# Dilated attention: each half of a query tile scored against its own three key tiles

## What is computed

```python
DILATED_GROUPS = ((128, 1), (512, 4), (2048, 16))   # window, dilation
for gi, (win, dil) in enumerate(DILATED_GROUPS):
    q, k, v = (to_residue(qkv[:, :, gi, n], dil) for n in range(3))
    o, lse = banded_attention(q, k, v, slopes, dil, win // (2 * dil), BLOCK_B)
wts = softmax(stack(lses), axis=0)
o = sum over the groups of wts * o, then  o @ w_out
# banded_attention: query t sees keys s with |s - t| <= window, logit bias -slope * dist_unit * |s - t|
```

## Time and profile before

| | |
|---|---|
| timed runs | 3117.51, 3118.22, 3127.80 us; median 3118.22 |
| profiled execution, its own time | 3128.69 us |
| its span | 3126.9 us |
| mean granted TensorE clock | 0.966 |
| busy over the span | PE 93%, PEld 75%, DVE 60%, ACT 41%, POOL 26% |
| the changed stage (785 to 1176 us) | 391 us, PE busy 379.5 us |

### The profile page before, as it was taken

The page is one execution under the profiler, slowest core; times in us unless marked ns, Lnnn a source line. Parts: engine busy times, 40 slices in busy tenths (PEclk is TensorE's granted clock), DMA queues, the critical chain, the costliest instruction groups (busy, mean ns, idle before and its releaser), DMA issues. The chain is left out here.

```text
span 3126.9 us, 54380 instructions
## 1 busy us (share of the span) xinstructions
PE 2899.3 (93%) x22377; PEld 2345.1 (75%) x22377; DVE 1873.7 (60%) x2647; ACT 1271.7 (41%) x1624; POOL 805.4 (26%) x461
## 2 busy tenths in 40 slices
PE   9899999999999989999979899769899799999994
PEld 8467888799777777888858677558786478888883
DVE  3766562201444445665256957685664779989997
ACT  3644332222333334332244321513222267777775
POOL 2013444344222212444400000010100024444531
PEclk9999999999999999999989899879999799999997
DMA  4633422322111112222222100321103379999996
GB/s 167 250 116 121 94 97 102 131 95 94 68 68 55 68 41 95 97 105 94 94 94 96 54 26 8 129 93 40 34 31 120 129 278 360 364 366 364 373 372 261
DMA packets 83393, 441.15 MB, mean 141 GB/s; under 512 B 19712, under 2 KB 22784, under 8 KB 34816
## 3 DMA queue, kind: packets, MB, share of 16 engines
q1 hardware_dynamic: 73920, 429.89, 37.7%
q0 software_dynamic: 9280, 8.43, 0.8%
HBM read 423.56 MB, written 37.77 MB: 148 GB/s over the span
## 5 line engine op out<-in xcount | busy, mean ns | idle before, releaser
L85 POOL TENSOR_TENSOR ring_lo<-ring,unit_hi 128x2048 fp32r<-128x2048 f32 x110 | 507.1, 4610 | 1066.1 <-ACT unit_hi L74 1066.1
L146 PE MATMUL wide<-h_hi,unit_hi 128*128 128x512 f32 x1296 | 515.6, 398 | 12.3 <-DVE h_lo L566 5.0
L147 PE MATMUL wide<-h_lo,unit_hi 128*128 128x512 f32 x1296 | 506.9, 391 | 0.0
L148 PE MATMUL wide<-h_hi,ring_lo 128*128 128x512 f32 x1296 | 506.6, 391 | 0.0
L3309 DVE TENSOR_TENSOR ex_w_lo<-ring,ex_w_hi 128x2048 fp32r<-128x2048 f32 x194 | 441.8, 2288 | 42.5 <-ACT ex_w_hi L3304 40.4
L3304 ACT CAST ex_w_hi<-ring 128x2048 fp32r<-128x2048 f32 x194 | 369.3, 1908 | 110.3 <-DMA ring<-in_weights 92.7
L74 ACT CAST unit_hi<-ring 128x2048 fp32r<-128x2048 f32 x114 | 217.7, 1910 | 386.9 <-PE wide L148 381.8
L146 PEld LDWEIGHTS wide<-h_hi,unit_hi 128*128 128x128 f32 x1296 | 244.5, 189 | 72.2 <-issue 13.6
L148 PEld LDWEIGHTS wide<-h_hi,ring_lo 128*128 128x128 f32 x1296 | 244.3, 189 | 52.3
L147 PEld LDWEIGHTS wide<-h_lo,unit_hi 128*128 128x128 f32 x1296 | 244.8, 189 | 48.7 <-issue 0.2
L391 DVE TENSOR_TENSOR ffn_hidden_lo<-ffn_whole,ffn_hidden_hi 128x512 f32 (+1 forms) x44 | 201.3, 4575 | 51.0 <-ACT ffn_hidden_hi L366 51.0
(11 more groups left out here) (560 smaller groups left out, 5911.3 us busy)
## 6 DMA issues: line engine op xcount, KB each, us to landing
ring<-in_weights SPq DMA_DIRECT2D x356, 1024.0 KB, 6.3
rw_F<-factors SPq DMA_DIRECT2D x8, 1024.0 KB, 6.5
factors<-rp_out SPq DMA_DIRECT2D x4, 1280.0 KB, 5.3
factors<-rp_out SPq DMA_DIRECT2D x4, 1024.0 KB, 5.4
ex_both<-pair_rows_out SPq DMA_DIRECT2D x4, 1024.0 KB, 7.8
x<-in_x SPq DMA_DIRECT2D x8, 256.0 KB, 7.6
x_kept<-x SPq DMA_DIRECT2D x1, 2048.0 KB, 13.1
x<-x_kept SPq DMA_DIRECT2D x1, 2048.0 KB, 7.9
```

The source lines that it names most:

```text
L85: pool.tensor_tensor(self.lo[n % RING][:, :], self.ring[n % RING][:, :], self.hi[n % 2][:, :].bitcast(F32), ALU.subtract).then_inc(self.lo ...
L146: pe.matmul(dst, a[0], b[0], start=start, stop=False)
L147: pe.matmul(dst, a[0], b[1], start=False, stop=False)
L148: return pe.matmul(dst, a[1], b[0], start=False, stop=stop)
```

## The change

The 128 queries of a tile are split into their first and last 64 (`side` 0 and 1). The first 64 are tokens below 256 and see only the key tiles 0 to 2 of group 0, the last 64 only the key tiles 1 to 3. So group 0 takes 384 score columns, another 384 for either side, and the scores, the probabilities and the table have 640 columns instead of 768. Each score product becomes two with 64 queries as weights, written to 64 partitions of the PSUM tile. The values of group 0 are multiplied with those query columns alone that can see the key tile (`near_queries`); the blocks of groups 1 and 2 come first and last, with all 128 queries.

```diff
-                    n = it.keys // P
-                    for t in range(n):
-                        for half in HALVES:
-                            m = pe.matmul(O[half * DH:(half + 1) * DH, 0:P], it.values[half][t], probT[:, half, t * P:(t + 1) * P],
-                                          start=(t == 0), stop=(t == n - 1))
+                    for n, parts in enumerate(it.values):
+                        for half, (value, t, first, last) in enumerate(parts):
+                            m = pe.matmul(O[half * DH:(half + 1) * DH, first:last], value, probT[:, half, t * P + first:t * P + last],
+                                          start=(n == 0), stop=(n == len(it.values) - 1))
...
-                            for half, (lhs, rhs, at) in enumerate(parts):
-                                m = pe.matmul(S(i, half)[:, at:at + rhs.shape[-1]], lhs, rhs, start=True, stop=True)
+                            for half, to, lhs, rhs, at in parts:
+                                m = pe.matmul(S(i, half)[to, at:at + rhs.shape[-1]], lhs, rhs, start=True, stop=True)
...
+NEAR = 3 * P
+WIDE_B = NEAR + 2 * P
+
+
+def near_queries(tile, side):
+
+    return max(side * DH, 32 * tile - 16), min((side + 1) * DH, 32 * tile + 48)
...
         for r in range(TT):
+            queries = [slice(r * P + side * DH, r * P + (side + 1) * DH) for side in range(2)]
             tile = slice(r * P, (r + 1) * P)
-            items.append(PairItem(heads, [slopes()[h] for h in heads],
-                                  dist[:, r, :],
-                                  [[(buf[s, 0, tile], buf[s, 1, :], 0) for s in rows],
-                                   [(buf[s, 2, tile], buf[s, 3, tile], T) for s in rows],
-                                   [(buf[s, 4, tile], buf[s, 5, tile], T + P) for s in rows]],
-                                  [[v[:, 0, t, at] for t in range(TT)] + [v[:, 1, r, at], v[:, 2, r, at]] for at in cols],
+            scores = [[(half, rows[side], buf[s, 0, queries[side]], buf[s, 1, side * P:side * P + NEAR], 0) for half, s in enumerate(rows) for side in range(2)]]
+            scores += [[(half, rows[side], buf[s, 2 * g, queries[side]], buf[s, 2 * g + 1, tile], NEAR + (g - 1) * P)
+                        for half, s in enumerate(rows) for side in range(2)] for g in (1, 2)]
+            values = [[(v[:, 1, r, at], 3, 0, P) for at in cols]]
+            values += [[(v[:, 0, block + side, at], block, *near_queries(block + side, side)) for at in cols] for block in range(3) for side in range(2)]
+            values += [[(v[:, 2, r, at], 4, 0, P) for at in cols]]
+            items.append(PairItem(heads, [slopes()[h] for h in heads], dist[:, r, :], scores, values,
                                   o[:, m, :].rearrange("p (i r) -> p r i", r=4)[:, r, :]))
...
-        whole_dist = ctx.enter_context(nc.sbuf_tensor("whole_dist", [P, TT, T + 2 * P], F32))
+        whole_dist = ctx.enter_context(nc.sbuf_tensor("whole_dist", [P, TT, WIDE_B], F32))
...
-    dist_b = np.empty((P, TT, T + 2 * P), np.float32)
+    dist_b = np.empty((P, TT, WIDE_B), np.float32)
     own = np.abs(i - np.arange(P)[None, :])
+    near = np.arange(NEAR)[None, :] + P * (i >= DH)
     for r in range(TT):
-        rel = np.abs(4 * i + r - np.arange(T)[None, :])
-        dist_b[:, r, :T] = np.where(rel <= 64, rel, FAR)
...
+        rel = np.abs(4 * i + r - near)
+        dist_b[:, r, :NEAR] = np.where(rel <= 64, rel, FAR)
```

More of the change, by code:

```diff
@@ L1049, in attention_a_items @@
             items.append(PairItem(heads, [slopes()[h] for h in heads], dist[:, off:off + keys],
-                                  [[(q[r, m, b * P:(b + 1) * P], k_[r, m // 4, first * P:last * P], 0) for r in rows]],
-                                  [[v[:, t, kv * DH:(kv + 1) * DH] for t in range(first, last)] for kv in kvs],
+                                  [[(half, slice(0, P), q[r, m, b * P:(b + 1) * P], k_[r, m // 4, first * P:last * P], 0) for half, r in enumerate(rows)]],
+                                  [[(v[:, t, kv * DH:(kv + 1) * DH], t - first, 0, P) for kv in kvs] for t in range(first, last)],
                                   o[:, m, b * P:(b + 1) * P]))
     return items
+NEAR = 3 * P
+WIDE_B = NEAR + 2 * P
+def near_queries(tile, side):
+    return max(side * DH, 32 * tile - 16), min((side + 1) * DH, 32 * tile + 48)
 def attention_b_items(qk, v, dist, o):
@@ L3731, in first_block @@
             qk = [sl(f"qk{i}", [P, 6, T]) for i in range(2)]
-            dist, scale = sl("dist_b", [P, TT, T + 2 * P], mybir.dt.bfloat16), sl("q_scale_b", [P, 2 * DC])[:, 0:DC]
+            dist, scale = sl("dist_b", [P, TT, WIDE_B], mybir.dt.bfloat16), sl("q_scale_b", [P, 2 * DC])[:, 0:DC]
             values_b_stage(nc, c, w, h, x, COLS["norm_mix1"], v,
@@ L3868, in distances @@
     dist_a = np.where(rel <= P, rel, FAR).astype(np.float32)
-    dist_b = np.empty((P, TT, T + 2 * P), np.float32)
+    dist_b = np.empty((P, TT, WIDE_B), np.float32)
     own = np.abs(i - np.arange(P)[None, :])
+    near = np.arange(NEAR)[None, :] + P * (i >= DH)
     for r in range(TT):
-        rel = np.abs(4 * i + r - np.arange(T)[None, :])
-        dist_b[:, r, :T] = np.where(rel <= 64, rel, FAR)
-    dist_b[:, :, T:T + P] = np.where(own <= 64, 4 * own, FAR)[:, None, :]
-    dist_b[:, :, T + P:] = np.where(own % 4 == 0, 4 * own, FAR)[:, None, :]
+        rel = np.abs(4 * i + r - near)
+        dist_b[:, r, :NEAR] = np.where(rel <= 64, rel, FAR)
+    dist_b[:, :, NEAR:NEAR + P] = np.where(own <= 64, 4 * own, FAR)[:, None, :]
+    dist_b[:, :, NEAR + P:] = np.where(own % 4 == 0, 4 * own, FAR)[:, None, :]
     return dist_a, dist_b
```

## The result

The changed kernel takes 3102.30 us (median of 8 runs, 3091.79 to 3108.74); the kernel before, with more runs, 3125.07 us (median of 8, 3117.51 to 3136.13). The ratio is 0.9916, 95% interval 0.9901 to 0.9931: 22 to 31 us faster. Two later comparisons of the same pair gave 0.9908 (0.9891 to 0.9924) and 0.9917 (0.9898 to 0.9937). The profiled execution's span is 3102.8 us against 3126.9.

The account below looks back on a forecast made before the run. TensorE was taken to bound the attention stage until its last four items, a chain of three engines. 16.8 us in the even part plus 4.7 at the end gave 21.5 us, from 3118.2 to 3097 us, range 3089 to 3111.

Parts of the forecast that it names:

- TensorE sets the even part: Stage up to item 28's scores: TensorE has no holes, so its savings shorten the stage one for one; 16.8 us.
- The scores: Score products of each item: four quarters cost one pass, 384 columns instead of 512; 1.23 us, 0.27 us saved.
- Scores with the quarters taking turns: Rival, scores: a row half's quarters alternate when streaming different keys; 2.31 us, 3130 us in all; chance 0.03 of 0.05.
- The values: Value products of each item: 12 narrow pairs at 0.058 us, set by weight loads; 1.28 us, 0.18 saved.
- The transposes: Transposes of each item: five instead of six a half, 0.22 us an item saved.
- The instructions: Matmul records on TensorE: 48 to 66 an item, 56 of them in 2.5 us; no cost taken.
- the rival of 62 ns of decoding per matmul: Scores and values: decoding binds, 0.48 us more an item, 13 us, 3131 us in all; chance 0.02.
- The wait for the copy: Projection chunk behind the values waits for VectorE's bank copy: 0.1 us seven times, 1.0 us with the first item's scores.
- The end of the stage: From item 28's scores on, a chain of three engines with shorter operations: 4.7 us saved.
- the 0.7 us that I had named and not counted: Last rounds: scores at 1146.79 ran at the lower clock; a shorter stall may lift that, 0.7 us, or move it.
- The sum: Whole kernel: 16.8 + 4.7 = 21.5 us saved, profiled execution 3128.7 to 3107.2 us, from the median 3097 us.
- two levels 10 us apart: Timed runs of the kernel before: it comes in two levels with no change, so savings were applied to the median 3118.2.

Follow-up runs that it names:

- the kernel that forces it: Changed kernel with both sides' scores written to the same 64 partitions, so a row half's two quarters can't run at once: one run 3140.96 us, stage 411.1 us.
- the split alone: Kernel before with only the scores split into 64 x 64 quarters, group 0 keeping 512 keys and the values six whole blocks: 3123.19 us, ratio 0.9988.
- the groups left whole: Changed kernel with groups 1 and 2 scored with all 128 queries as weights, only group 0 in quarters: 3107.47 us, ratio 0.9949 to the kernel before.
- one more step of 0.23 us an item: Changed kernel with the last 64 queries' key tiles ordered 3, 1, 2: 3094.07 us, ratio 0.9888; with transposes also ahead of the second chunk 3094.35 us, 0.9889.

## Why the prediction was right

**TensorE sets the even part: right.** It is busy all of it before and after, cutting the other engines' work alone left the period at 51.31 us, and 0.65 us fewer on TensorE an item (0.26 for the scores, 0.17 for the values, 0.22 for the transposes) gave a period of 48.75 us. Expected 48.7.

**The scores: right.** Predicted 1.23 us, measured 1.243. Scores with the quarters taking turns were put at 2.31 us, and the kernel that forces it has 2.36. The 0.21 and 0.15 us for a turn with 128 and 64 columns of weights came out of subtraction; the split alone confirms the difference (1.456 against 1.503), the groups left whole the turn itself (0.21).

**The values: right.** Predicted 1.28, measured 1.287 us. That a narrow pass goes by its weights and not its columns was taken from 36-column matmuls with 128-column weights; it holds from 64 down to 16 columns with 64-column weights, in that the columns don't matter.

**The transposes: right.** They take 0.11 us less a half.

**The instructions: right.** 56 matmuls in 2.53 us show no cost, so the rival of 62 ns of decoding per matmul falls: 24 score matmuls in 1.24 us are 52 ns each, 32 value matmuls in 1.29 us 40 ns.

**The wait for the copy: right place, too dear.** I had 0.1 us seven times. The copy of this round after the change,

```profile
937.70 1.18 DVE L1110 SCALAR_TENSOR_TENSOR qk<-wide,q_scale_b,rstd 128x512 f32<-128x512 f32 x1 [2.74 <-PE wide L148]
```

ends at 938.88 and the chunk starts at 938.93: the signal takes 0.05 us, not 0.1, and the values blocks of the even part lose 0.3 us in sum. The first item's scores lost 0.23 us, as expected, and those of the third item another 0.1, which I hadn't named. The even part gained 16.6 us (to the start of item 28's scores 354.7 before, 338.1 after) against the 16.8 of the sum. That it is so near is in part luck: without waits the blocks gain 17.3 us, 0.5 less than the 17.8 of the sum, and the waits cost 0.65 us, 0.35 less than the 1.0 put against it.

**The end of the stage: right, with the clock on top.** The operations came out at 0.822, 0.824 and 0.691 us against 0.82, 0.82 and 0.69. The first chain round went from 7.25 to 6.32 us (0.93, predicted 0.97), the third from 4.42 to 3.78 (0.64, predicted 0.67), the rest from 18.98 to 16.88 (2.10, predicted 2.1). The second went from 7.92 to 6.31: its scores ran at the lower clock before and at full clock after, the 0.7 us that I had named and not counted. Together 5.3 us against 4.7. Those 0.7 us are a matter of the profile: in the third profile of the changed kernel TensorE's clock is at half for 3.4 us in this round, which takes 6.66 us. Without them the stage's gain is 21.2 us.

**The sum: 21.5 predicted, 21.9 in the stage, 22 to 31 in the ratio.** The gain was forecast right. The forecast of 3097 us against the measured 3102.3 has another error in it. I took three timed runs (3117.5, 3118.2 and 3127.8 us) for two levels 10 us apart and subtracted from the lower. The eight runs of the kernel before lie at 3117.5, 3118.2, 3123.3, 3124.4, 3125.8, 3127.8, 3129.4 and 3136.1 us: one spread, no two levels, with a median of 3125.07. From there 21.5 us give 3103.6.

What lies between the stage's gain and the ratio's is in part behind the stage. The longest stretch of the recurrent mixer, which the change doesn't touch, in profiles of the kernel before:

```profile
2041.90:2393.00 351.10, 301.57 (x9169) 270.48 (x9169) 212.16 (x498) 87.19 (x217) 33.16 (x71) 0.96 0.10 37
```

```profile
2044.40:2391.90 347.50, 301.90 (x9168) 271.31 (x9168) 212.53 (x498) 87.16 (x217) 33.06 (x71) 0.96 0.11 37
```

and of the kernel after:

```profile
2023.50:2370.90 347.40, 302.14 (x9169) 271.75 (x9169) 212.34 (x498) 87.14 (x217) 33.16 (x71) 0.96 0.11 37
```

```profile
2017.70:2358.70 341.00, 300.17 (x9168) 270.55 (x9169) 212.20 (x498) 87.25 (x217) 33.34 (x71) 0.95 0.11 38
```

The third profile of the changed kernel has 341.4 us, the split alone (768 columns) 346.3. So three profiles with 768 columns average 348.3 us and three of the changed kernel 343.3. That is the size of the rest, but the same kernel moves by 6 us there from one profile to the next. Over all thirteen profiles the nine kernels and repeats with 640 score columns on TensorE have 338.8 to 347.4 us (mean 343.4), the four with 768 columns 346.3 to 351.2 (mean 349.0): two groups that overlap only a little. The length goes with TensorE's idle time for which the profile shows no releaser ("issue"): 9.5 us of it in the shortest of these stretches, 18.5 and 17.4 in the two longest. What makes that idle time longer or shorter isn't shown. The experts vary by 8 us from one profile to the next (616.1 to 624.6 for the changed kernel alone).

There is one more place for a part of the rest. The kernel before has 393.3 us in its stage in one profile and 395.0 in the other, with more time at half clock, and the timed runs without a profile may have either. So whether the mixer gains from the change is open: no experiment tells it, and no mechanism is in sight.

## What to carry to other kernels

Splitting a matmul into quarters of the array costs nothing as long as all four are kept busy at once; it pays by the columns that each quarter needn't stream. Split its neighbours too, even where they save nothing, if that spares a turn of the array (0.21 us here). Up to 64 columns of f32 with 64-column weights, count passes and not columns: lay data out so that one weight block meets all its queries in one pass. And when a block between a product and the next use of its bank gets shorter, look at what its length was hiding: in one more step of 0.23 us an item, half was lost to a 1.17 us copy until other work was moved in front of it.

## What the runs showed of the hardware

- Four 64 x 64 quarters run at the pace of one, also where the two of a row half stream different operands (the passes of 384 columns, 0.32 us): 24 passes of 384 and 128 columns take 1.24 us, and 2.36 us when both sides are written to the same 64 partitions.
- A pass of 16 columns takes as long as one of 64, 0.058 us, with 64 columns of f32 weights.
- In the last rounds TensorE stands idle for over 2 us, waiting for a copy of a transposed tile, and in some profiles its granted clock falls to half for 3.4 us about 1.5 us behind the end of the first such wait. It did so in both profiles of the kernel before (idle 2.64 us; clock 0.95 and 0.91 over these rounds) and in one of the three of the changed kernel, though all three have the same idle time of 2.35 us. In the profile with the shortest wait, 2.05 us where only the other engines' work was cut, it stayed at 1.00. That a shorter wait spares the clock isn't shown.
- Two profiles of the changed kernel differ by 13 us behind a stage of 371.4 us in both (1943.8 and 1930.8 us): 6.4 us in the mixer's stretch, 3.1 in the experts, the rest between the stage and the mixer.
